# Cleared products in one stretch and a shared emptying of the transposed x at the start of a decoder step

## The reference

```
sh1, sc1, gt1, sh2, sc2, gt2 = split(silu(c) @ w_mod + b_mod, 6)
h = rmsnorm(x, g_pre_mix) * (1 + sc1) + sh1
aq, af, ai, ag, bq, bk, bv, gate_a, gate_b = split(h @ w_in)
o_a = hgrn2(aq, af, ai, ag); o_b = differential_attention(bq, bk, bv)
merged = sigmoid(gate_a) * (o_a @ w_proj_a) + sigmoid(gate_b) * (o_b @ w_proj_b)
x = x + gt1 * rmsnorm(merged @ w_out, g_post_mix)
h2 = rmsnorm(x, g_pre_ffn) * (1 + sc2) + sh2
x = x + gt2 * rmsnorm(moe(h2), g_post_ffn)        # top 4 of 32 clamped-SwiGLU experts
```

## Time and profile before

| what | value |
|---|---|
| span of the profiled execution | 1258.5 us |
| device time, median of three runs | 1261.01 us (1259.24 to 1261.58) |
| PE busy | 1102.0 us, 88% of the span |
| DVE busy | 588.2 us, 47% |
| ACT busy | 230.7 us, 18% |
| HBM read | 479.47 MB, 385 GB/s over the span |

### The profile page before, as it was taken

How to read it: one execution, slowest core, us unless ns; L and a number is a source line. 1 busy time by engine, 2 the same in 40 slices (tenths; PEclk the granted TensorE clock), 3 DMA queues, 4 the chain that set the end, 5 groups by cost and what they waited for, 6 DMA issues and landing times.

```text
span 1258.5 us, 23992 instructions
## 1 busy us (share of the span) xinstructions
PE 1102.0 (88%) x9856; PEld 456.6 (36%) x9856; DVE 588.2 (47%) x1166; ACT 230.7 (18%) x420; POOL 68.5 (5%) x126
## 2 busy tenths in 40 slices
PE   8999999999988697996887979999966995667996
PEld 4776777785322131321222322333211331112332
DVE  3536744444654252563353544666532552332654
ACT  3002510141311110220111211112100211100212
POOL 0312020250100000000000000000000000000000
PEclk9999999999989897998798999999988998888999
DMA  9979994599899999999999999999999999999995
GB/s 342 312 245 347 317 339 154 187 384 366 284 428 429 426 429 426 429 425 429 426 428 428 428 426 393 409 424 427 428 427 428 427 426 430 424 431 425 428 428 236
DMA packets 67619, 485.30 MB, mean 386 GB/s; under 512 B 6421, under 2 KB 29450, under 8 KB 40762
## 3 DMA queue, kind: packets, MB, share of 16 engines
q1 hardware_dynamic: 59312, 461.07, 88.9%
q0 software_dynamic: 7104, 19.65, 4.9%
q10 hardware_dynamic: 1130, 3.51, 0.8%
HBM read 479.47 MB, written 4.72 MB: 385 GB/s over the span
## 4 chain that ended last, share of the span: by engine, by line
DMA 45%; PE 27%; DVE 1%; issue 0%; DVEq 0%; ACT 0%; ACTq 0%
DMA big<-in_w_down 26%; PE PB L1247 13%; DMA big<-in_w_gate_up 13%; PE PB L1274 7%; DMA hTG<-in_w_down 5%; PE PB L1214 2%; PE PB L1201 2%; PE PB L1206 1%; PE PB L1229 1%; PE PB L1221 1%; PE PB L1240 0%; PE PB L1186 0%; PE PB L1232 0%; DVE big L1623 0%; DVE big L1620 0%
## 5 line engine op out<-in xcount | busy, mean ns | idle before, releaser
L1247 PE MATMUL PB<-big,cst 128*32 128x512 f32 x2768 | 355.0, 657 | 109.2 <-DMA big<-in_w_gate_up 109.2
L2189 DVE TENSOR_TENSOR tok<-PB,cst 32x512 f32<-32x512 f32 x188 | 129.1, 687 | 261.7 <-ACT cst L1554 259.8
L1247 PEld LDWEIGHTS PB<-big,cst 128*32 128x32 f32 x2768 | 89.0, 115 | 345.2 <-issue 181.1
L1274 PE MATMUL PB<-big,cst 128*32 128x512 f32 x1408 | 166.6, 602 | 12.8 <-DMA big<-in_w_down 12.7
L2165 DVE TENSOR_SCALAR mod<-PB 64x256 f32<-64x256 f32 x96 | 41.0, 427 | 209.1 <-PE PB L1247 208.4
L756 PE MATMUL PB<-hTG,big 128*128 128x264 f32 x576 | 136.5, 391 | 0.4 <-DVE hTG L1617 0.4
L756 PEld LDWEIGHTS PB<-hTG,big 128*128 128x128 f32 x576 | 106.9, 190 | 27.3 <-issue 10.8
L1544 ACT ACTIVATE mod<-PB 64x256 f32<-64x256 f32 x96 | 36.1, 376 | 422.3 <-PE PB L1247 421.7
L1274 PEld LDWEIGHTS PB<-big,cst 128*32 128x32 f32 x1408 | 39.2, 110 | 96.8 <-issue 65.8
L1201 PE MATMUL PB<-wide,att 128*32 128x256 f32 x784 | 57.9, 415 | 5.1 <-DVE att L2159 4.9
L1554 ACT ACTIVATE cst<-PB 128x512 f32<-128x512 f32 x48 | 28.7, 597 | 178.2 <-PE PB L1274 178.2
(11 more groups left out here) (378 smaller groups left out, 970.9 us busy)
## 6 DMA issues: line engine op xcount, KB each, us to landing
big<-in_w_gate_up SPq DMA_DIRECT2D x115, 2048.0 KB, 31.0
big<-in_w_down SPq DMA_DIRECT2D x57, 2048.0 KB, 23.9
hTG<-in_w_gate_up SPq DMA_DIRECT2D x13, 2048.0 KB, 37.1
big<-in_w_mod SPq DMA_DIRECT2D x24, 1024.0 KB, 7.5
big<-in_w_in SPq DMA_DIRECT2D x22, 1024.0 KB, 9.2
hTG<-in_w_down SPq DMA_DIRECT2D x6, 2048.0 KB, 24.0
wide<-in_cache_k POOLq DMA_DIRECT2D x16, 256.0 KB, 6.8
big<-in_w_out SPq DMA_DIRECT2D x4, 1024.0 KB, 10.5
```

The lines of the kernel that those rows point to most:

```text
L1247: mm = pe.matmul(GU[32 * j:32 * j + 32, :], mo["xT"][:, (2 * u + r) * M:(2 * u + r + 1) * M], groups(w[:, r * 2 * D:(r + 1) * 2 * D])[:, j ...
L1274: mm = pe.matmul(DN[32 * j:32 * j + 32, :], mo["actT"][:, (4 * u + r) * M:(4 * u + r + 1) * M], w[:, r * D + half * 512:r * D + (half + 1) ...
L2189: mm = dve.tensor_tensor(mo["y"][rows, :], DN[rows, :], mo["y_part"][other, :], ALU.add)
```

## The change

Three things. The cleared products of the beginning, 6, 4 and 7, become 17, 5 and 2: 17 ahead of the transpose "vt", 24 in place of 17 in all. ACT empties only the banks of even k of the transposed x. DVE empties those of odd k, between making `xn` and copying the scale rows; after each copy it waits until the bank of k-1 is freed, and then frees its own.

```diff
             pe.wait_ge(S("zeros_ready"), 1)
-            idle_products(6)
+            idle_products(17)
             pe.wait_ge(S("small_loaded"), 16 * 8)
...
-            idle_products(4)
+            idle_products(5)
             scale_bias()
-            idle_products(7)
+            idle_products(2)
             scale_part(0)
...
-            for k in range(KC):
+            for k in range(0, KC, 2):
                 act.wait_ge(S("aux_full"), AUX[f"xt{k}"] + 1)
                 act.wait_ge(S("aux_free"), AUX[f"xt{k}"])
                 do(act.activation(hT[:, k, :], aux(f"xt{k}")[:, 0:T], ACT.Copy))
...
             dve.nop().then_inc(S("xn_ready"), 1)
+            for k in range(1, KC, 2):
+                copy(hT[:, k, :], bank(f"xt{k}")[:, 0:T])
+                dve.wait_ge(S("aux_free"), AUX[f"xt{k}"])
+                dve.nop().then_inc(S("aux_free"), 1)
```

## The result

The change takes 1265.09 us in the median of 12 runs (1263.14 to 1272.23), the kernel before 1260.53 (1259.15 to 1266.39). The ratio is 1.0037, 95% interval [1.0022, 1.0052], so 2.8 to 6.6 us more. The shortest run of the change, 1263.14, is longer than ten of the twelve of the kernel before. The forecast was 1260.3 us, with a range up to 1262.6; the result lies outside it.

A forecast was written before the change was run, and what follows sets the result against it. PE bounds the front to 340 us, the experts' weight DMA the rest. x_T(0) -0.15, first four transposes -0.54, emptying 0: -0.7 us, span 1257.8; plus 2.5 to the median, 1260.3 us, range 1258.5 to 1262.6.

The forecast's parts named there:

- "vt": Transpose at PE's head, behind 17 cleared products: forecast at 7.8 us, ends 6.83 and 8.72, 3.4 us late.
- xn: Ready on ACT and DVE at 15.35 us (14.4 to 16.3), putting x_T(0) there in place of 15.51: -0.15 us.
- The clock's rise: PE's beginning: the unbroken 17 cleared products raise the clock from 1.2 to 2.4 GHz, taking between 5.3 and 6.9 us.
- The waits: PE waiting for w_mod units before the first two scale parts: some 0.6 us before 11.08, 1.5 before 13.64.
- the first four take 2.09 too: First four x_T transposes on PE: with the clock up, 2.09 us in place of 2.63, -0.54 us.
- the prediction's own signs of being wrong: Seventeen products at 7.2 us, a second scale part of 1.94, or in_T moving by more than 1.6 us either way.
- Rival 2: Slower: clock rises, then falls again before PE's transposes; 0 to +2.7 us, taken as +1.0, 1262.0 us; chance 0.18.
- Rival 1: Slower: cleared products at PE's head don't raise the clock; x_T(0) at 16.5, +1.0 us, 1262.0; chance 0.20.
- Rival 3: More gained: in other executions of the kernel before the clock rises later; change saves 2.2 us, 1258.8; chance 0.12.
- The emptying in turn: ACT and DVE alternately emptying the banks of transposed x: PE does not wait, 0 us, bounds -0.3 and +0.2.
- The passing on: From in_T through the front and the experts to the end: any shift of in_T arrives almost whole.
- rival 4: Nothing arrives: PE is on time, but a transfer (shift pieces, a gather) holds it; 1261.0 us; chance 0.08.

The follow-up runs named there:

- the last version: Kernel before with cleared products 6, 12, 8 and 5 (five between the first two scale parts), 96 rows each, ACT alone emptying: ratio 1.0015.
- the first four experiments: In order told: products regrouped alone, on the kernel before, 1.0033; emptying in turn alone, likewise, 1.0006; the change with both waits filled, 1.0004; with only the second filled, 1.0005.

## Why the prediction was wrong

- **"vt": right; xn: forecast a little too late.** "vt" at 7.09 (7.8 forecast; ends 6.83 and 8.72), `xn` at 14.23 (15.35, ends 14.4 to 16.3, so just outside). The three products more cost nothing.
- **The clock's rise: right.** The 17 products took 5.76 us, inside the 5.3 to 6.9 that were to show it. The Trainium skill's rule ("TensorE: Matmul & The Clock Gate", "What's actually happening"), that activity releases the throttled level, held for this stretch, and the row that spoke against it was one of a stretch with breaks.
- **The waits: the first too small, and both wrong in what they do.** 0.6 and 1.5 us were foreseen, 1.46 and 1.49 came, and they were taken as harmless cover ("that saving goes into a wait"). The forecast carried the ends of "vt" to `xn`, but not to the first wait, though an earlier "vt" lengthens it: with "vt" at 6.83 the same sum gives 1.6 us.
- **This is the step that failed:** "With the clock up from the start the first four take 2.09 too", priced at -0.54. The clock was up at the start and down again from 12.3, and everything to 25.8 ran low: the first four took 3.28, +0.65, and the rest behind them lost 2.93 more. With either wait filled the ratio is that of the kernel before within the noise (1.0005 and 0.9991); the products alone bring the loss (1.0033). Two of the prediction's own signs of being wrong came: a second part of 1.93 us, and an `in_T` that moved by more than 1.6 us.
- **Rival 2 was the mechanism, with its place and its test,** a part at 13.64 of 1.94 us. It was given a chance of 0.18 and +1.0 us. Its worst end, +2.7, was still short: it counted one of the two parts that run among the transposes; with the second's 0.87 it comes to 3.6, against 3.58 measured. The Trainium skill's rule cited there (same page, "HAM oscillation — how this bites in real kernels"), that a waiting PE falls back, agrees with the trace: 1.00 to 12.2 us, 0.50 behind, though the waits in the page's example are longer than the ones here. The break of 0.40 us held against it was a single one, behind busy products, and no measure for one of 1.46. A better row stood in the same trace, in the expert phase, where the earlier trace rows has a PEclk of 0.93. PE of the kernel before, in order of time:

```profile
397.74 1.92 PE L1247 MATMUL PB<-big,cst 128*32 128x512 f32 x16 [1.35 <-DMA big<-in_w_gate_up]
402.62 3.57 PE L1247 MATMUL PB<-big,cst 128*32 128x512 f32 x16 [2.96 <-DMA big<-in_w_gate_up]
```

Two waits of 1.35 and 2.96 us stand around 16 products of 1.92 us, and behind them 16 products of the same shape take 3.57 us; the PEclk column is 1.00 from 398 to 402.5 and 0.50 from 402.6 to 405.9.

- **Rival 1** (no rise) did not happen to the change, but to the last version, with 96 rows and a break at "vt".
- **Rival 3** had the spread the other way round: the beginning does differ between executions, but the profiled one of the kernel before was not a good one (23.02 in the run with its products unchanged). What makes its long runs (6 of 35 above 1265 us on the chip of the first four experiments) stays open.
- **The emptying in turn: nothing,** as priced.
- **The passing on: right for a loss** (+3.57 became +3.44 and +3.2), **too generous for a gain.** From `in_T` to SP's first weights -1.78 became -0.82, -1.75 became -1.07, -1.36 (second wait filled) became -0.58 and -0.97 (first wait filled) became +0.28. The gathered sample values and DVE take the rest where I looked, in part rival 4.
- **From span to time** the forecast added 2.5 us, the distance from one execution's span to the median. Each profiled execution with both on record has 1.7, so the profiled one of the kernel before took some 1260.2 us (an estimate), near its median of 1260.53; 0.8 us of the sum was the choice of execution.

## What to carry to other kernels

Work that only keeps the clock up belongs where PE would otherwise wait, not in one lump ahead of the waits: a faster PE waits longer for the same DMA, and here the clock won was lost there, with everything behind at the low level. Price such a fall over all work to the next rise, every transpose and part in it, and not by the wait alone. Even so, the filled versions only came back to the time of the kernel before. And before trusting one profile of a beginning of 25 us, ask whether the rise of the clock is in the same place in another execution.

## What the runs showed of the hardware

- The granted clock fell from 1.00 to 0.50 around waits of PE far shorter than the stretch that it then stayed low: in the change by 12.3 us, behind a wait of 1.46 us, 1.07 us of matmuls and 0.1 us of the next wait; in the products alone by 12.9, behind 0.94 us, 1.07 us of matmuls and 0.9 us of wait; in the kernel before with 128 rows by 11.2, behind 2.48 us and 0.3 us of matmuls. Where the longest wait ahead of a part was 0.36 to 0.78 us (three runs) it stayed up.
- Once down, it stayed at 0.50 through some 12 us of transposes and scale parts with hardly a gap (13.64 to 25.8 in the change). In the kernel before it rose in such a run, during the first four transposes.
- Cleared products of 96 and of 128 rows take the same time at the same level (six take 2.74 us, and 2.74 with 128 rows), but behind six of 128 rows and "vt" the clock was up by 4.83 us (1.03 us for four) where behind six of 96 rows it was not (1.91 us).
- In the change's own trace the PEclk column shows the fall (0.50); ahead of the first rise it shows 1.00 at the low level too, as from 7.49 to 11.08 in the earlier trace rows, where seven products take 3.17 us.
